# A decoder layer on one core: the third token tile scaled before the sample tile's norm, two weight copies moved ahead on ScalarE, and two low parts on VectorE

## The reference

```python
merged = jax.nn.sigmoid(ga) * y_a + jax.nn.sigmoid(gb) * y_b
x = x + g1[:, None] * rmsnorm(merged @ w_out, norm_post1)

h2 = rmsnorm(x, norm_pre2) * (1 + sc2[:, None]) + sh2[:, None]
a, gt = jnp.split(h2 @ w_up, 2, axis=-1)
a_conv, ffn_buf_new = causal_dwconv(a, ffn_buf, ffn_conv_w, ffn_conv_b)
f = (jax.nn.gelu(a_conv) * gt) @ w_down
x = x + g2[:, None] * rmsnorm(f, norm_post2)
```

## Time and profile before

| | us |
|---|---|
| median of 3 runs | 1033.81 |
| lowest and highest | 1032.07, 1036.01 |
| the profiled execution's own time | 1034.1 |
| its span, first to last instruction | 1032.4 |
| PE busy | 1006.8 (98%) |
| DVE, ACT, POOL busy | 455.4, 368.5, 350.6 |

### The profile page before, as it was taken

One profiled execution on the slowest core, in us unless ns is written; L12 is line 12 of the kernel. 1 busy time (PEld: TensorE's weight loads), 2 busy tenths in 40 slices (PEclk: granted clock), 3 DMA queues, 4 the chain that ended last, 5 costly groups with the idle time before them and its releaser, 6 DMA issues.

```text
span 1032.4 us, 19214 instructions
## 1 busy us (share of the span) xinstructions
PE 1006.8 (98%) x7823; PEld 912.9 (88%) x7823; DVE 455.4 (44%) x664; ACT 368.5 (36%) x556; POOL 350.6 (34%) x175
## 2 busy tenths in 40 slices
PE   6899999999999999999999989999999999999997
PEld 4499889999999999999988789999999999888886
DVE  2401104575666554534556757544444444300204
ACT  4432533143434342544463424333333333212212
POOL 2033433242433333323450214433333333333330
PEclk9899999999999999999999989999999999999999
DMA  9657333656664566545462113322222222222222
GB/s 354 165 81 183 116 87 89 138 98 139 171 163 121 139 150 104 129 103 128 129 204 72 39 44 96 89 81 81 81 81 81 81 81 81 83 81 82 83 69 91
DMA packets 144113, 115.33 MB, mean 112 GB/s; under 512 B 11353, under 2 KB 123761, under 8 KB 143025
## 3 DMA queue, kind: packets, MB, share of 16 engines
q1 hardware_dynamic: 143953, 114.38, 42.1%
q10 hardware_dynamic: 96, 0.04, 0.0%
HBM read 107.02 MB, written 7.35 MB: 111 GB/s over the span
## 4 chain that ended last, share of the span: by engine, by line
PE 93%; SPq 3%; DVE 1%; ACT 1%; issue 1%; DMA 0%; DVEq 0%
PE pair L1549 61%; PE pair L1601 16%; PE pair L1875 4%; SPq L587 2%; PE pair L1681 1%; PE pair L1654 1%; PE pair L1536 1%; SPq L625 1%; PE pair L1593 1%; PE pair L1744 1%; PE pair L1733 1%; PE pair L1594 1%; PE pair L1595 1%; PE pair L1592 1%; PE pair L1788 1%
## 5 line engine op out<-in xcount | busy, mean ns | idle before, releaser
L765 POOL TENSOR_TENSOR w_lo<-raw,w_hi 128x1024 fp32r<-128x1024 f32 x108 | 263.3, 2440 | 501.5 <-ACT w_hi L831 501.5
L1549 PE MATMUL pair<-h_hi,w_hi 128*128 128x288 f32 x1568 | 348.5, 301 | 6.7 <-issue 4.0
L1549 PE MATMUL pair<-h_hi,w_lo 128*128 128x288 f32 x1568 | 342.0, 296 | 0.0
L1549 PE MATMUL pair<-h_lo,w_hi 128*128 128x288 f32 x1568 | 341.6, 296 | 0.0
L1549 PEld LDWEIGHTS pair<-h_hi,w_hi 128*128 128x128 f32 x1568 | 254.9, 189 | 25.3 <-issue 20.9
L1549 PEld LDWEIGHTS pair<-h_lo,w_hi 128*128 128x128 f32 x1568 | 255.2, 189 | 0.0
L1549 PEld LDWEIGHTS pair<-h_hi,w_lo 128*128 128x128 f32 x1568 | 255.2, 189 | 0.0
L831 ACT ACTIVATE w_hi<-raw 128x1024 fp32r<-128x1024 f32 x110 | 116.1, 1057 | 172.4 <-PE pair L1595 97.3
L765 POOL TENSOR_TENSOR w_lo<-raw_c,w_hi 128x1024 fp32r<-128x1024 f32 x24 | 66.7, 2782 | 128.3 <-ACT w_hi L831 128.3
L442 DVE SCALAR_TENSOR_TENSOR cv<-ext,ffp,cv 128x592 f32<-128x592 f32 x44 | 82.8, 1882 | 5.7 <-DVE cv L439 3.0
L1601 PE MATMUL pair<-w_hi,f_hi 128*128 128x512 f32 x176 | 68.8, 391 | 0.0
(11 more groups left out here) (306 smaller groups left out, 1132.8 us busy)
## 6 DMA issues: line engine op xcount, KB each, us to landing
raw<-in_w_up SPq DMA_DIRECT2D x44, 512.0 KB, 3.8
raw<-in_w_in SPq DMA_DIRECT2D x256, 64.0 KB, 3.2
raw_c<-in_w_ada SPq DMA_DIRECT2D x32, 512.0 KB, 5.7
raw_c<-in_w_in SPq DMA_DIRECT2D x192, 64.0 KB, 3.9
raw<-in_w_down SPq DMA_DIRECT2D x22, 512.0 KB, 3.5
ada_first<-in_w_ada SPq DMA_DIRECT2D x8, 1024.0 KB, 13.6
raw<-in_w_in SPq DMA_DIRECT2D x8, 512.0 KB, 5.2
s_in<-in_state_gla SPq DMA_DIRECT2D x16, 256.0 KB, 4.2
```

The source lines that it names most:

```text
L765: pool.tensor_tensor(lo, raw_tile(n)[:, :], hi.bitcast(F32), ALU.subtract).then_inc(S("w_lo_done"), 1)
L1549: ins = pe.matmul(bank[pair][:, half, 0:HALF], w[:, i, :], x[:, i, HALF * half:HALF * half + HALF], start=i == 0 and p == 0, stop=i == KT ...
```

## The change

ScalarE: at the sample tile (x = 3), the copy of up tile 72 goes between the sample copy and the wait for the sum. The copy of tile 73 follows the root, then `h2_high(2)` goes ahead of `x_stats(3)`. At x = 4, the copies of tiles 74 and 75 both come ahead of `x_stats(4)`; tile 75's was in `ffn_up(0)`, behind both last `h2_high`.

VectorE: the low parts of tiles 72 and 73 are made here (`up_low`), around a new order at x = 3: `y_sum(3)`, `up_low(0)`, `h2_scale(2)`, `h2_shift(2)`, `y_part(3)`, `up_low(1)`, `h2_low(2)`, `xn_part(3)`.

GpSimd: it starts the up tiles with 74, after VectorE's two.

TensorE: `to_channels(2)` comes after the first `w_out` tile of the last product instead of the second; `to_channels(4)` moves from before (2, 0) into its middle.

```diff
         def y_stats(x, between=()):
...
                 act.activation(y_smp[:, :], pair[64:P, :], ACT.Copy).then_inc(S("y_smp"), 1)
+                for n in between:
+                    high(n)
                 act.wait_ge(S("y_smp"), 2)
...
         for x in range(TT):
-            y_stats(x)
+            y_stats(x, (TILE_UP,) if x == TT - 2 else ())
             if x == TT - 2:
-                high(TILE_UP)
                 high(TILE_UP + 1)
+                h2_high(x - 1)
+                x_stats(x)
+                continue
             if x == TT - 1:
                 high(TILE_UP + 2)
+                high(TILE_UP + 3)
             x_stats(x)
...
-            with pool.Fori(TILE_UP // 4, TILES // 4) as g:
+            pool.wait_ge(S("w_lo_done"), TILE_UP + 2)
+            for n in (TILE_UP + 2, TILE_UP + 3):
+                low(n, w_hi[n % 4][:, :], w_lo[n % 4][:, :], n + 1)
+            with pool.Fori(TILE_UP // 4 + 1, TILES // 4) as g:
...
-                    high(n + 3, i)
+                    if e == 1 or not isinstance(i, int) or i > 0:
+                        high(n + 3, i)
...
+            def up_low(i):
+                dve.wait_ge(S("w_hi_done"), TILE_UP + i + 1)
+                dve.wait_ge(S("w_lo_done"), TILE_UP + i)
+                dve.tensor_tensor(w_lo[i][:, :], raw_tile(TILE_UP + i)[:, :], w_hi[i][:, :].bitcast(F32),
+                                  ALU.subtract).then_inc(S("w_lo_done"), 1)
...
-                    if MIXED[x] == NCH:
+                    if x == TT - 2:
                         y_sum(dve, x)
+                        up_low(0)
+                        h2_scale(dve, x - 1)
+                        h2_shift(dve, x - 1)
+                        y_part(dve, x)
+                        up_low(1)
+                        h2_low(dve, x - 1)
+                        xn_part(dve, x)
+                        continue
...
-                    if x == TT - 1 and y == 1:
+                    if x == TT - 1 and y == 0:
                         to_channels(x - 2)
...
-                if half == 0 and e in (1, 2):
-                    to_channels(TT - 3 + e)
+                if half == 0 and e == 1:
+                    to_channels(TT - 2)
...
+                if (e, half) == (2, 0):
+                    channel_tile(kc(w_hi[e]), kc(w_lo[e]), e, (h_hi, h_lo), 0, (half,))
+                    to_channels(TT - 1)
+                    channel_tile(kc(w_hi[e]), kc(w_lo[e]), e, (h_hi, h_lo), 1, (half,))
```

More of the change, by code:

```diff
@@ L385, in act_out, with y_stats @@
     def act_out(act, high):
-        def y_stats(x):
+        def y_stats(x, between=()):
             t, pair = MIXED[x], flat(wo_pair(x))
@@ L1912, in _ @@
                         pe.wait_ge(S("y_scaled"), (3, 5, 4)[e])
-                channel_tile(kc(w_hi[e]), kc(w_lo[e]), e, (h_hi, h_lo), token_halves=(half,))
+                if (e, half) == (2, 0):
+                    channel_tile(kc(w_hi[e]), kc(w_lo[e]), e, (h_hi, h_lo), 0, (half,))
+                    to_channels(TT - 1)
+                    channel_tile(kc(w_hi[e]), kc(w_lo[e]), e, (h_hi, h_lo), 1, (half,))
+                else:
+                    channel_tile(kc(w_hi[e]), kc(w_lo[e]), e, (h_hi, h_lo), token_halves=(half,))
             with pe.Fori(1, FT // 2) as i:
```

## The result

| | before | changed |
|---|---|---|
| median of 6 runs, us | 1034.37 | 1026.18 |
| lowest, highest | 1032.07, 1036.33 | 1024.30, 1026.74 |
| the profiled execution's own time, its span | 1034.1, 1032.4 | 1026.71, 1025.0 |

Ratio 0.9926, 95% interval 0.9906 to 0.9947: faster by 0.7%. A second measurement of the same kernel gave 0.9925 (0.9909 to 0.9940). Forecast was 1025.9 us.

A forecast was written before the change was run, and what follows sets the result against it. TensorE, busy 98% of the span, was taken as the bound. Removing pauses of 2.86 and 4.16 us and their slow clock, less new waits of 1.3 and 0.3, gave 8.2 us off 1034.1: 1025.9 us, range 1023.0 to 1030.5.

The forecast's parts named there:

- One for one: TensorE from 628 is always busy at 2.4 GHz, so time won before (0, 1) comes off the end in full.
- The second pause and "issue": TensorE before (3, 0): the wait called "issue" is for GpSimd's low part of tile 75; gain 4.16 + 1.4 us.
- The first pause: TensorE before (0, 0), waiting for the third token tile's `h_lo`: pause and slow clock go, gain 2.86 + 1.4 us.
- The last token tile: VectorE's add and shift meet GpSimd's subtractions, giving back 1.3 us in (2, 0) and 0.3 us before (0, 1).
- Add held up by low 74: VectorE, last token tile: the add from 594.4 meets GpSimd's subtraction of tile 74 and ends 1.09 us behind it, 597.4.
- Pause in (2, 0): TensorE, middle of (2, 0): it stands 1.3 us, from 599.95, until the last token tile's `xn` at 601.25.
- The last wait, before (0, 1): TensorE waits another 0.3 us for the fourth product's input, ready at 607.2; (0, 1) starts at about 607.3.
- rival 2: GpSimd does tiles 74 and 75 together ahead of VectorE's add; pause of 2.4 us in (2, 0), gain 6.2 us; chance 0.10.
- The clock: TensorE's clock was taken to hold at full speed through the new 1.3 us pause in (2, 0).
- rival 3: TensorE's clock falls in the new 1.3 us pause: 12 to 24 slow matmuls, gain 7.2 to 6.0 us; chance 0.18.
- ScalarE's copy of 75: ScalarE at x = 4: the copy waits for its load, about 593.5, and ends at 594.8, before `x_stats(4)` is due at 595.7.
- rival 5: Copy of tile 75, ahead of `x_stats(4)`, blocks ScalarE waiting for a DMA: gain 0 or below, 1034 us and up; chance 0.02.

The follow-up runs named there:

- e1: Kernel before with only the copy of up tile 75 moved ahead of `x_stats(4)`: 18.81 us from product's end to (0, 1), before 24.28; ratio 0.9933.
- e2: Changed kernel with the copy of tile 75 back behind the last `h2_high`: 22.89 us from product's end to (0, 1), changed 15.95; ratio to before 0.9992.
- e3: Changed kernel with low parts of tiles 72 and 73 on GpSimd again, new order kept: 16.28 us from product's end to (0, 1); ratio to before 0.9923.
- e5: Changed kernel with the old order at x = 3, low parts of 72 and 73 still on VectorE: 15.95 us from product's end to (0, 1).
- e8: Changed kernel with old order at x = 3 and low parts of 72 and 73 on GpSimd: 18.93 us from product's end to (0, 1); ratio 0.9948.
- e6: Changed kernel with the copy of tile 74 ahead of `y_stats(4)`: 14.70 us from product's end to (0, 1), changed 15.95; ratio to before 0.9871.
- e4: Changed kernel with the last transposes ahead of (2, 0) again, (2, 0) in one piece: 18.70 us from product's end to (0, 1); ratio to before 0.9944.
- e7: Changed kernel with GpSimd's subtraction of tile 75 also waiting for the last `xn`: 15.02 us from product's end to (0, 1), changed 15.95.

## Why the prediction was right

*One for one.* After (0, 1) 417.0 against 416.9 us: what is won before it comes off the end. Right.

*The second pause and "issue".* Right, shown by e1 and e2: that move alone takes 5.5 of the 8.3 us, and without it the pause is back, named. The reading rested on 0.1 us between the end of GpSimd's row and TensorE's start, in the face of the profile's own word.

*The first pause.* Size right: `h_lo` ended 0.55 us before the product (0.4 forecast). The account of it was incomplete. I had credited the low parts on VectorE and the new order together; e3, e5 and e8 show that one of the two is enough (0.3, 0.0 and 3.0 us more than changed). What the title's first edit (the order) buys is nothing while the third (the low parts on VectorE) stands, and the third buys 0.3 us while the first stands.

*The last token tile.* Right, its terms too. Add held up by low 74: forecast to end 6.2 us behind the product's end, measured 6.2 (598.20). `xn`: 10.05 forecast, 9.87 measured. Pause in (2, 0): 1.3 forecast, 1.3 between the starts at 600.61 and 601.93 less one pace, 1.2. The last wait, before (0, 1): 0.3 forecast, 0.29 measured (607.54, one pace, 607.96). (0, 1): 16.1 forecast, 15.95 measured. The add got in between the two subtractions, as at 587.19, so rival 2 did not happen. The Trainium skill (SBUF — State Buffer, Who interferes with whom) says that a VectorE instruction with two SBUF inputs contends with a GpSimd one that reads SBUF, and one with at most one such input outside the two-port modes doesn't. The runs agree: in e6 the scale out of PSUM takes 0.68 beside a subtraction, the shift right behind it 2.18 instead of 0.69; in e3 the sample tile's scale, with `y_smp` in SBUF, takes 3.23 instead of 1.28.

*The clock* held at 1.00 through the pause of 1.2 us and behind it (rival 3 did not happen). Behind 2.7 us in e4, 2.6 in e8 and 2.84 in e1 the granted clock of the next 3 us was 0.51, 0.50 and 0.50. The prediction let twelve matmuls lose behind each pause of the kernel before; the rows have 11 and 13, the same in all.

*ScalarE's copy of 75* (rival 5) waited for its load 0.57 us in e6, where nothing else hid it, and that cost nothing: ScalarE then still stood idle for 1.18 us before `x_stats(4)`.

*Total.* 8.2 forecast, 8.3 by the trace, and 8.2 between the medians. The trace's figure is the firm one. That the median fell within 0.3 us of the forecast is in part luck: the prediction knew nothing of two paces 6.5 us apart, and both profiles happened to have the slower one.

## What to carry to other kernels

When two engines share a way to memory, count for every operation where its inputs lie and who works beside it: here 1.2 us adds took 3.0, and a later start of the other's work (e7) or an earlier one (e6) was worth 0.9 to 1.3 us. A chain that waits should be followed through the cross-engine copy that feeds it, even where the profile names no releaser. And two edits that each remove the same pause don't add: try one of them alone before both are kept.

## What the runs showed of the hardware that I had not expected

The up loop's matmuls run at one of two paces, at granted clock 1.00 in both. These are two executions over the same stretch of 200 us, the changed kernel, then e5, with the columns of the earlier trace rows.

```profile
640.00:840.00 200.00, 200.00 (x1502) 200.00 (x1501) 104.12 (x176) 65.11 (x127) 76.81 (x32) 1.00 0.29 84
```

```profile
640.00:840.00 200.00, 200.00 (x1541) 200.00 (x1540) 104.21 (x180) 66.80 (x129) 78.42 (x34) 1.00 0.30 86
```

1502 and 1541 matmuls are 0.1332 and 0.1298 us each. Over the loop's 1920 matmuls (40 tiles of 48) that is 6.5 us, and it shows: from (0, 1) to the end of the span it took 410.5 us in e1 and 410.6 in e5, and 416.9 to 417.0 in before, changed, e2, e3, e4, e6, e7 and e8. The scatter of one kernel is of this size: in 31 executions the kernel before took 1026.0 to 1036.1 us. The pace is 6.5 of these 10; another part lies ahead of (0, 0): the end of the `w_out` product falls anywhere from 589.15 to 592.47 in the profiles, though no edit lengthens that product. So I take the pace to change from execution to execution, but this is argued from times: no kernel was profiled at both paces. Nor is it shown that an edit leaves the odds alone: by their times, eight of ten runs of e1 had the quicker pace and none of twelve of the changed kernel. In the first measurement the six runs of the kernel before lay within 4.3 us and those of the changed one within 2.4, with no overlap, and the trace, at the same pace in both, gives the same difference, so the verdict isn't touched. What sets the pace stays open; no run here varied it.

The number of slow matmuls after a pause isn't fixed: 11 to 14 behind pauses of 2.6 to 2.9 us and of 4.2 us, 24 behind 5.7 us in e2. The Trainium skill (TensorE: Matmul & The Clock Gate, What's actually happening) gives 6, 11 or 14 for one kernel; e2's 24 lie outside that, and the estimate in the prediction (0.7 to 1.5 us for one return) would have been too low there, where it cost 2.6.
